# Second weight units of four streams, loaded and split into buffers of their own during the preceding stage

## The chip, the cores and the metric

One core of a Trainium2 chip runs the whole program in one launch. The metric is the device time in microseconds, the median of several runs. The engines named in the rows: PE is TensorE (matrix products), PEld its weight loads, DVE VectorE, ACT ScalarE, POOL GpSimd, SP SyncE (here it only issues DMAs).

## What is computed

Two blocks over 512 tokens of width 1024, in float32:

```python
h = x
for l in range(2):
    hn = rms_norm(h, norm_mix_pre[l])
    # l = 0: gated linear recurrence; l = 1: windowed attention with shared keys and values
    mixed = concat([y, memory_attention(mq, mk, mv)]) @ w_out[l]
    h = h + rms_norm(mixed, norm_mix_post[l])
    f = swiglu_ffn(rms_norm(h, norm_ffn_pre[l]), w_ffn_in[l], w_ffn_out[l])   # 1024 -> 2 x 2816 -> 1024
    h = h + rms_norm(f, norm_ffn_post[l])
    if l == 0:
        kv = rms_norm(h, norm_kv) @ w_kv_shared        # keys: first half, values: second half
# second block: modulation from silu(c) @ w_ada, then x_m, z, u = h @ w_in_2,
# an mLSTM and a Fourier mix, @ w_out_2, and a mixture of 16 experts
```

Every product is made of three passes in a rounded format: each operand is split into a high part (rounded) and a low part (the rest), and high x high, high x low and low x high are added.

## The kernel before

Weights stream through two slots. One half unit is 128 x 1024 numbers (512 KB). `load_half` (SyncE) brings it to `ring[s]`, `split_high` (ScalarE) rounds it to `weights_high`, `split_low` (VectorE) subtracts to get `weights_low`, and TensorE uses both in 24 matmuls of 512 columns. Slot s is 0 or 1; `landed[s]`, `high_done`, `split_done` and `used_done` are the semaphores, counted in one order over all halves: a slot is split again when the half before it in the same slot is used, and loaded again when that half is split. Each engine carries out its instructions in the order in which the Python code writes them.

`stream` runs a stage: units i with halves s = 0 and 1. For each half it writes load and split, then the evacuation of unit i - 1, then what is given as `beside(i, s)`, then TensorE's products, then, in the feed-forward stages, one or two sums of the modulation (`modulation_sum`, eight VectorE instructions on 128 x 128). `then` opens the next stage's first unit behind the last products.

The order of the stages: mixer 0 (its output rows by `mix_out`, 8 rows), feed-forward 0 (`ffn`: a stream of 22 units of w_ffn_in, then the stream of 22 rows of w_ffn_out in 11 units), the shared keys and values, queries of layer 1, attention, `mix_out` again, feed-forward 1, then z and u (4 units of w_in_2) and the rest of the second block. A stage of rows ends with `rows_root`: bank 0 is copied (`kept`), ScalarE squares the eight banks as `chunk_done` comes in, VectorE adds them, TensorE sums over features by one-column matmuls, and the root is spread. Then `Residual.chunks` adds the residual, and scales and splits X chunk by chunk, while TensorE makes the products of the next stage's first unit, both halves at once (the paired or fused first unit). `Residual.root` and `Residual.spread` make the next root; its copy `rstd` is what evacuations multiply by.

So the first unit of such a stage holds both slots until its end, and unit 1 can be split only then. In a feed-forward stage unit 1 is filled as a pair (`fused and i == 1`), the root is spread between its halves, and unit 0 is evacuated behind its second half (`evacuate(0, both)`: gate product on L1192, silu on L1196, product on L1203, high part on L1207, low part on L1210). Behind the keys the values use both slots in `token_products`, where tokens are the output rows, and then layer 1's first unit waits for them. For z and u, `both_columns` makes the first unit (L1651).

The modulation's weights go through `ring[2]` and `ring[3]` by GpSimd's queue (`modulation_load`), first at 175 us, and then each time one has been summed.

## Time and profile before

| what | value |
|---|---|
| median of 3 runs | 1953.93 us (1953.65 to 1957.99) |
| span of the profiled execution | 1947.3 us |
| TensorE busy | 1814.3 us (93%) |
| VectorE busy | 1216.2 us (62%) |
| ScalarE busy | 896.1 us (46%) |
| mean DMA rate | 149 GB/s |

The span runs from the first to the last instruction of one profiled execution; the device time of a run has some microseconds around it. Busy time of TensorE is not the same as work at its peak. The chain that ended last, followed back from the end, tells which engine's work the end hung on, and the timelines around a joint tell which wait ended last there. Matmuls are pipelined, so that their pitch is the distance of two starts and not the length of one.

### The profile page before, as it was taken

What the parts mean: (1) busy time and instruction counts of PE and PEld (TensorE: products, weight loads), DVE (VectorE), ACT (ScalarE), POOL (GpSimd) and SP (SyncE); (2) the same over time, 40 slices, a digit from 0 to 9 for tenths busy, and PEclk for the clock granted to TensorE, in tenths of its full rate; (3) what the DMA queues carried; (4) which work ended last, traced back from release to release, by engine and by line L of the source; (5) the groups of instructions that cost most, each with busy time, mean ns of one, the idle gap of its engine ahead of it and who ended that gap; (6) DMA issues with size and microseconds to landing.
All of it is one profiled execution on the core that took longest, in us unless ns stands there. A gap on an engine that the chain in (4) does not pass through costs nothing.

```text
span 1947.3 us, 25641 instructions
## 1 busy us (share of the span) xinstructions
PE 1814.3 (93%) x9201; PEld 1507.9 (77%) x9201; DVE 1216.2 (62%) x2170; ACT 896.1 (46%) x1452; POOL 125.7 (6%) x137
## 2 busy tenths in 40 slices
PE   7997999999999997899999999799987989999997
PEld 7875788888887865678888888678576878888885
DVE  3554668887323656456865532564575479889888
ACT  3446443222213445543223221342383368888885
POOL 1000000000000000000110000120000210110102
PEclk8898999999999998999999999799998879999999
DMA  4223225455333124024655423330011359999995
GB/s 150 87 76 115 87 64 142 134 145 147 107 96 96 44 65 184 23 65 137 182 159 149 119 93 97 112 89 22 21 67 66 108 222 377 395 385 370 386 372 187
DMA packets 203854, 289.32 MB, mean 149 GB/s; under 512 B 12332, under 2 KB 150548, under 8 KB 203636
## 3 DMA queue, kind: packets, MB, share of 16 engines
q1 hardware_dynamic: 188788, 239.56, 36.9%
q0 software_dynamic: 11920, 36.48, 6.1%
q10 hardware_dynamic: 3056, 12.06, 1.6%
q8 instruction: 59, 0.97, 0.2%
q14 instruction: 31, 0.25, 0.0%
HBM read 271.77 MB, written 21.53 MB: 151 GB/s over the span
## 4 chain that ended last, share of the span: by engine, by line
PE 85%; DVE 7%; ACT 6%; issue 1%; DMA 1%; POOL 0%; DVEq 0%; ACTq 0%; POOLq 0%
PE bank L200 23%; PE bank L202 23%; PE bank L201 23%; PE bank L69 11%; PE bank L654 2%; DVE weights_low L227 1%; PE bank L2195 1%; ACT weights_high L221 1%; DVE tmp L69 1%; DVE z_and_u L69 1%; DVE ring L69 1%; PE bank L1651 1%; ACT spare L69 1%; PE bank L2544 1%; PE bank L272 1%
## 5 line engine op out<-in xcount | busy, mean ns | idle before, releaser
L227 DVE TENSOR_TENSOR weights_low<-ring,weights_high 128x1024 fp32r<-128x1024 f32 x202 | 246.7, 1223 | 395.3 <-ACT weights_high L221 394.8
L200 PE MATMUL bank<-XH,weights_high 128*128 128x512 f32 x1056 | 423.2, 401 | 17.8 <-DVE weights_low L227 6.5
L202 PE MATMUL bank<-XH,weights_low 128*128 128x512 f32 x1056 | 415.6, 394 | 0.0
L201 PE MATMUL bank<-XL,weights_high 128*128 128x512 f32 x1056 | 415.2, 393 | 0.0
L221 ACT CAST weights_high<-ring 128x1024 fp32r<-128x1024 f32 x202 | 211.1, 1047 | 432.6 <-PE bank L202 422.8
L200 PEld LDWEIGHTS bank<-XH,weights_high 128*128 128x128 f32 x1056 | 200.8, 190 | 63.0 <-DVE weights_low L227 9.6
L202 PEld LDWEIGHTS bank<-XH,weights_low 128*128 128x128 f32 x1056 | 200.7, 190 | 43.4
L201 PEld LDWEIGHTS bank<-XL,weights_high 128*128 128x128 f32 x1056 | 201.1, 190 | 40.3 <-issue 0.5
L2235 DVE TENSOR_TENSOR XL<-ring,XH 128x1024 fp32r<-128x1024 f32 x144 | 169.8, 1219 | 11.7 <-ACT XH L2229 11.7
L2229 ACT CAST XH<-ring 128x1024 fp32r<-128x1024 f32 x144 | 145.2, 1048 | 0.6 <-PE bank L202 0.6
L69 DVE SCALAR_TENSOR_TENSOR squares<-ring,c_silu,squares 128x128 f32<-128x128 f32 x384 | 135.2, 352 | 13.6
L200 PE MATMUL bank<-hidden_high,weights_high 128*128 128x512 f32 x352 | 137.1, 390 | 0.0
L202 PE MATMUL bank<-hidden_high,weights_low 128*128 128x512 f32 x352 | 137.0, 389 | 0.0
L201 PE MATMUL bank<-hidden_low,weights_high 128*128 128x512 f32 x352 | 136.9, 389 | 0.0
L189 POOL DMA_DIRECT2D ring<-in_w_ada x48 | 42.5, 885 | 711.9 <-DVE squares L263 711.9
L2235 DVE TENSOR_TENSOR weights_low<-ring,weights_high 128x1024 fp32r<-128x1024 f32 x72 | 86.0, 1216 | 0.0
L1196 ACT ACTIVATE tmp<-tmp 128x512 f32<-128x512 f32 x44 | 27.8, 632 | 109.2 <-DVE tmp L1192 109.1
L202 PEld LDWEIGHTS bank<-hidden_high,weights_low 128*128 128x128 f32 x352 | 66.1, 188 | 13.8
L201 PEld LDWEIGHTS bank<-hidden_low,weights_high 128*128 128x128 f32 x352 | 66.1, 188 | 13.8
L200 PEld LDWEIGHTS bank<-hidden_high,weights_high 128*128 128x128 f32 x352 | 66.1, 188 | 13.4
L200 PE MATMUL bank<-weights_high,gathered_high 128*128 128x256 f32 (+1 forms) x216 | 70.8, 328 | 3.6 <-DVE weights_low L2235 1.8
L2229 ACT CAST weights_high<-ring 128x1024 fp32r<-128x1024 f32 x72 | 74.1, 1053 | 0.0
(506 smaller groups left out, 3263.2 us busy)
## 6 DMA issues: line engine op xcount, KB each, us to landing
ring<-in_w_ffn_in SPq DMA_DIRECT2D x88, 512.0 KB, 4.7
ring<-in_w_gate SPq DMA_DIRECT2D x72, 512.0 KB, 5.4
ring<-in_w_up SPq DMA_DIRECT2D x72, 512.0 KB, 7.3
ring<-in_w_down SPq DMA_DIRECT2D x72, 512.0 KB, 5.9
ring<-in_w_ada POOLq DMA_DIRECT2D x48, 512.0 KB, 4.7
ring<-in_w_ffn_out SPq DMA_DIRECT2D x44, 512.0 KB, 3.6
ring<-in_w_out SPq DMA_DIRECT2D x24, 512.0 KB, 3.6
slot_output<-expert_out SPq DMA_DIRECT2D x18, 512.0 KB, 6.7
```

The source lines that it names most:

```text
L69: op(*args, **kw).then_inc(self.line.sem, 1)
L189: queue.eng.dma_start(dst, src).then_inc(ln.sem, 16)
L200: PE.matmul(out_ap, w_h, x_h, start=first, stop=False, skip_group_check=True)
L201: PE.matmul(out_ap, w_h, x_l, start=False, stop=False, skip_group_check=True)
L202: return PE.matmul(out_ap, w_l, x_h, start=False, stop=last, skip_group_check=True)
L221: S.copy(wh[:, s, :], ring[s][:, :]).then_inc(high_done.sem, 1)
L227: V.tensor_tensor(wl[:, s, :], ring[s][:, :], wh[:, s, :].bitcast(F32), ALU.subtract).then_inc(split_done.sem, 1)
L272: t = PE.matmul(bank[7][:, 2 * n + j:2 * n + j + 1], ada_acc(n, j), ones[:, 0:1], start=True, stop=True, skip_group_check=True)
L654: return PE.matmul(bank[s][:, cols], w[:, s, k * P:(k + 1) * P], x[:, k, cols], start=start, stop=stop, skip_group_check=True)
L1196: S.activation(sg, sg, ACT.Silu).then_inc(silu_done.sem, 1)
L2229: S.copy(high[s], raw[q]).then_inc(l_high.sem, 1)
L2235: V.tensor_tensor(low[s], raw[q], high[s].bitcast(F32), ALU.subtract).then_inc(l_split.sem, 1)
```

## The change

A class `Early` holds a pair of buffers (high and low, at a fixed address) for unit 1 of a stream, or, for the values, for their only unit. Its `load` puts the two halves into `ring[2]` and `ring[3]` on SyncE, and its `split` rounds and subtracts one half behind the waits given. `stream` takes `early`: unit 1 is then not filled, its products read these buffers, and unit 2 is opened in the slots at once (in the feed-forward stages ahead of the two evacuations of unit 0). The waits on slots count per slot (`slot_used`, `slot_split`), since uses no longer alternate. Where and behind what it is done:

- feed-forward 0: loaded ahead of mixer 0's output rows, split at (3, 0) and (3, 1), the last two of its eight rows. The first two modulation loads move behind these splits.
- values: loaded at (8, 0) of feed-forward 0's rows, split at (10, 0) and (10, 1), the last two of 22. Modulation loads 20 and 21 move to the next item.
- feed-forward 1: loaded ahead of mixer 1's output rows, split at (2, 0) and (2, 1).
- z and u: loaded at (8, 0) of feed-forward 1's rows behind `used_done.now()`, split at (9, 1) and (10, 0); the additions of the position stay in their place (given as `beside` now and no longer as an evacuation).

In `rows_root`, `split_low(0)` moves ahead of the additions of the squares.

```diff
-            g = high_done.n
             S.wait_ge(landed[s].sem, landed[s].n)
-            if g >= 2:
-                S.wait_ge(used_done.sem, g - 1)
+            if slot_used[s]:
+                S.wait_ge(used_done.sem, slot_used[s])
...
+            slot_split[s] = split_done.n
+
+        def slots_used(*each):
+
+            for s in each:
+                used_done.n += 1
+                slot_used[s] = used_done.n
+
+        def wait_slots(*each):
+
+            PE.wait_ge(split_done.sem, max(slot_split[s] for s in each))
+
+        class Early:
+
+
+            def __init__(self, name, src, unit, at):
+                self.src, self.unit = src, unit
+                self.high, self.low = (nc.alloc_sbuf_tensor_at(f"{name}_unit_{x}", [P, 2, HALF], F32R, offset=at + 2 * HALF * 4 * n)
+                                       for n, x in enumerate(("high", "low")))
+                self.high_line, self.split_line = line(f"{name}_high_done"), line(f"{name}_split_done")
+
+            def load(self, *after):
+                sp.need(*after)
+                for s in range(2):
+                    ap, view = self.src(self.unit, s)
+                    load(sp, landed[2 + s], view(ring[2 + s][:, :]), ap)
+
+            def split(self, s, *after):
+                act.need(*after)
+                S.wait_ge(landed[2 + s].sem, landed[2 + s].n)
+                S.copy(self.high[:, s, :], ring[2 + s][:, :]).then_inc(self.high_line.sem, 1)
+                self.high_line.n += 1
+                V.wait_ge(self.high_line.sem, self.high_line.n)
+                V.tensor_tensor(self.low[:, s, :], ring[2 + s][:, :], self.high[:, s, :].bitcast(F32),
+                                ALU.subtract).then_inc(self.split_line.sem, 1)
+                self.split_line.n += 1
...
-                    if i == 0 and s in opened:
+                    if s in opened:
                         opened.remove(s)
                     elif fused and i == 1:
                         if s == 0:
-                            fill_half(src, i, 0)
-                            fill_half(src, i, 1)
+                            if not early:
+                                fill_half(src, i, 0)
+                                fill_half(src, i, 1)
                             fused.root()
-                    else:
+                    elif not (early and i == 1):
...
+                            wait_slots(0, 1)
                             paired()
-                            used_done.n += 2
+                            slots_used(0, 1)
+                    elif early and i == 1:
+                        PE.wait_ge(early.split_line.sem, s + 1)
+                        products(i, s, False, early).then_inc(used_done.sem, 1)
+                        used_done.n += 1
+                        if not fused:
+                            open_half(src, s, 2)
                     else:
-                        PE.wait_ge(split_done.sem, used_done.n + 1)
+                        wait_slots(s)
                         products(i, s, i == 0).then_inc(used_done.sem, 1)
-                        used_done.n += 1
+                        slots_used(s)
                     if fused and i == 1:
                         if s == 0:
                             fused.spread()
                         else:
                             for both in range(2):
+                                if early:
+                                    open_half(src, both, 2)
                                 evacuate(0, both, used_done.n - 2)
...
-                            if n + 2 < 48:
+                            if n + 2 < 48 and n + 2 not in (20, 21):
...
+                PE.wait_ge(early.split_line.sem, 2)
+            else:
+                wait_slots(0, 1)
+            w_h, w_l = (early.high, early.low) if early else (wh, wl)
...
+                split_low(0)
             added, squared = {}, {}
             for c in range(KC):
                 if c == 0:
@@ -564,7 +617,6 @@
                     added[c] = vec.do(V.tensor_tensor, total, total, squares[c % 4], ALU.add,
                                       after=[squared[c], added[c - 1]])
             if next_src:
-                split_low(0)
...
+            if i == 3:
+                early.split(s, used_done.now(), vec.line.now())
         load(pool, tables_landed, con[:, P:], I["constants"][:, P:], after=[used_done.now()])
         pool.need(used_done.now())
+        unit_at = 191616
+        early = Early("first_ffn", ffn_src(0), 1, unit_at)
+        early.load(used_done.now())
+        spread = mix_out(I["w_out"][0], ffn_src(0), row_order, row_ready, row_part)
+        G.wait_ge(early.split_line.sem, 2)
         modulation_load(0)
         modulation_load(1)
-        spread = mix_out(I["w_out"][0], ffn_src(0), row_order, row_ready, row_part)
         a_ctx.close()
-        spread = ffn(0, Residual(column["mix_post0"], spread, column["ffn_pre0"], True), columns_src(I["w_kv_shared"]))
+        value_src = columns_src(I["w_kv_shared"], base=KV_HEADS * DH)
+        values_early = Early("values", value_src, 0, 204416)
+
+        def split_values(i, s):
+            if (i, s) == (8, 0):
+                values_early.load((ada_summed, ada_sums[19]))
+            if i == 10:
+                values_early.split(s, used_done.now())
+        spread = ffn(0, Residual(column["mix_post0"], spread, column["ffn_pre0"], True), early, columns_src(I["w_kv_shared"]),
+                     split_values)
...
-        fill_half(value_src, 0, 0)
-        fill_half(value_src, 0, 1)
...
-        spread = mix_out(I["w_out"][1], ffn_src(1), row_order, row_ready)
+        early = Early("second_ffn", ffn_src(1), 1, unit_at)
+        early.load(used_done.now(), values_early.split_line.now())
+
+        def split_early(i, s):
+            if i == 2:
+                early.split(s, used_done.now())
+        root_table()
+        spread = mix_out(I["w_out"][1], ffn_src(1), row_order, row_ready, split_early)
+        G.wait_ge(early.split_line.sem, 2)
+        modulation_load(20)
+        modulation_load(21)
...
+        zu_early = Early("z_and_u", zu_src, 1, 149632)
+
+        def positions_and_early(i, s):
+            if i:
+                add_position(i - 1, s, None)
+            if (i, s) == (8, 0):
+                zu_early.load(used_done.now(), (ada_summed, ada_summed.n))
+            if i in (9, 10):
+                if (i, s) in ((9, 1), (10, 0)):
+                    zu_early.split(2 * i + s - 19, used_done.now())
+        spread = ffn(1, Residual(column["mix_post1"], spread, column["ffn_pre1"], True), early, zu_src, positions_and_early)
...
-            stream(4, zu_src, columns_products(T, XH, XL), zu_and_context, then=opener(in2_src), paired=both_columns)
+            stream(4, zu_src, columns_products(T, XH, XL), zu_and_context, then=opener(in2_src), paired=both_columns, early=zu_early)
```

## Rows read from the trace of the kernel before

**Rows 1.** The page's chain that ended last: shares of the span by engine.

```profile
PE 85%; DVE 7%; ACT 6%; issue 1%; DMA 1%; POOL 0%; DVEq 0%; ACTq 0%; POOLq 0%
```

**Rows 2.** The chain in order of time, first feed-forward: start us, us, what.

```profile
256.16 0.79 PE bank L69 x8
```

**Rows 3.** Timeline of PE, first feed-forward: start, us, instruction, [idle before <-releaser].

```profile
261.45 0.95 PE L69 MATMUL bank<-ones,squares 128*128 128x1 f32 x8
262.71 0.50 PE L200 MATMUL bank<-XH,weights_high 128*128 128x512 f32 x1 [0.31 <-DVE weights_low L227]
...
276.03 0.39 PE L202 MATMUL bank<-XH,weights_low 128*128 128x512 f32 x1
277.23 0.50 PE L200 MATMUL bank<-XH,weights_high 128*128 128x512 f32 x1 [0.81 <-DVE weights_low L227]
...
288.05 0.39 PE L202 MATMUL bank<-XH,weights_low 128*128 128x512 f32 x1
```

**Rows 4.** VectorE's timeline and its waits (in total, times, longest), 271.5 to 287.9.

```profile
271.60 0.69 DVE L1192 TENSOR_TENSOR tmp<-bank,rstd 128x512 f32<-128x512 f32 x1 [7.31 <-ACT rstd L69]
...
286.62 1.22 DVE L227 TENSOR_TENSOR weights_low<-ring,weights_high 128x1024 fp32r<-128x1024 f32 x1
...
DVE hidden_low L1210 <- ACT hidden_high L1207: 1.4, 2, 0.7
DVE tmp L1203 <- ACT tmp L1196: 1.3, 1, 1.3
DVE weights_low L227 <- ACT weights_high L221: 0.3, 1, 0.3
```

**Rows 5.** Timeline of ScalarE, VectorE and PE around the first mixer's root.

```profile
228.39 1.05 ACT L221 CAST weights_high<-ring 128x1024 fp32r<-128x1024 f32 x1 [4.39 <-PE bank L202]
229.01 0.69 DVE L69 COPY spare<-bank 128x512 f32<-128x512 f32 x1 [3.76 <-PE bank L202]
...
233.70 1.49 DVE L69 TENSOR_TENSOR tmp<-tmp,squares 128x512 f32<-128x512 f32 x2
...
235.62 1.31 PE L69 MATMUL bank<-ones,tmp 128*128 128x1 f32 x8
```

**Rows 6.** Around the values: timeline (long rows) and chain (short rows).

```profile
650.56 0.95 PE L69 MATMUL bank<-ones,squares 128*128 128x1 f32 x8
653.26 0.55 PE L200 MATMUL bank<-weights_high,XH 128*128 128x256 f32 x1 [1.76 <-DVE weights_low L227]
...
660.69 1.29 DVE L69 TENSOR_TENSOR rotated<-bank,const_tables 128x512 f32<-128x512 f32 x2
...
667.00 0.13 PE bank L202
...
669.57 0.50 PE bank L200
```

**Rows 7.** The chain around z and u.

```profile
1275.95 2.73 PE bank L1651 x12
...
1281.13 0.50 PE bank L200
```

**Rows 8.** Second feed-forward's last rows: ScalarE's timeline, one load's landing, and a stretch.

```profile
1207.31 1.05 ACT L221 CAST weights_high<-ring 128x1024 fp32r<-128x1024 f32 x1 [4.39 <-PE bank L202]
...
DMA to landing us min/median/max: 3.8/3.8/3.8
...
1228.00:1228.50 0.50, 0.50 (x4) 0.42 (x3) 0.00 (x0) 0.00 (x0) 0.00 (x0) 1.00 1.01 307
```

**Rows 9.** Stretches: us, busy (x) of PE, PEld, DVE, ACT, POOL, granted clock, DMA share, GB/s.

```profile
263.70:267.10 3.40, 3.40 (x9) 2.62 (x9) 0.56 (x3) 0.00 (x0) 0.00 (x0) 0.52 0.85 235
653.00:656.20 3.20, 2.94 (x14) 2.97 (x15) 3.20 (x7) 3.20 (x6) 0.00 (x0) 0.52 0.89 264
881.50:884.70 3.20, 3.20 (x9) 2.49 (x8) 0.69 (x3) 0.00 (x0) 0.00 (x0) 0.50 0.81 228
667.20:669.50 2.30, 0.78 (x2) 0.00 (x0) 1.22 (x2) 2.29 (x4) 0.00 (x0) 1.00 0.00 0
1278.70:1281.10 2.40, 1.33 (x6) 0.76 (x5) 1.23 (x1) 2.33 (x3) 0.00 (x0) 1.00 0.00 0
```

More of the change, by code:

```diff
@@ L288, in opener, with stream @@
             return lambda s: open_half(src, s)
-        def stream(units, src, products, evacuate=None, side=None, then=None, fused=None, beside=None, paired=None):
+        def stream(units, src, products, evacuate=None, side=None, then=None, fused=None, beside=None, paired=None, early=None):
             pending = []
@@ L379, in columns_products, with products @@
         def columns_products(n, xh, xl, to=0, ready=None):
-            def products(i, s, first):
-                w_h = wh[:, s, :].rearrange("p (k n) -> p k n", k=KC)
-                w_l = wl[:, s, :].rearrange("p (k n) -> p k n", k=KC)
+            def products(i, s, first, halves=None):
+                high, low = (halves.high, halves.low) if halves else (wh, wl)
+                w_h = high[:, s, :].rearrange("p (k n) -> p k n", k=KC)
+                w_l = low[:, s, :].rearrange("p (k n) -> p k n", k=KC)
                 b = to + 4 * (i % 2) + s
@@ L393, in columns_products, with token_products @@
             return products
-        def token_products(tiles, xh, xl, to=0, between=None):
+        def token_products(tiles, xh, xl, to=0, between=None, early=None):
             for a in range((tiles + 1) // 2):
                 pe.need(*bank_free[to + a])
-            PE.wait_ge(split_done.sem, used_done.n + 2)
+            if early:
+                PE.wait_ge(early.split_line.sem, 2)
+            else:
+                wait_slots(0, 1)
+            w_h, w_l = (early.high, early.low) if early else (wh, wl)
             for m in range(tiles):
@@ L404, in token_products @@
                     x_h, x_l = xh[:, k, m * P:(m + 1) * P], xl[:, k, m * P:(m + 1) * P]
-                    last = three_pass(dst, x_h, x_l, wh[:, :, k * P:(k + 1) * P], wl[:, :, k * P:(k + 1) * P],
+                    last = three_pass(dst, x_h, x_l, w_h[:, :, k * P:(k + 1) * P], w_l[:, :, k * P:(k + 1) * P],
                                       k == 0, k == KC - 1)
@@ L409, in token_products @@
             last.then_inc(used_done.sem, 2)
-            used_done.n += 2
+            if early:
+                used_done.n += 2
+            else:
+                slots_used(0, 1)
         def rows_products(units, xh, xl, ready=None, order=None, tokens=None, between=None):
@@ L693, in chunks @@
                             pe.need(*bank_free[0], *bank_free[1])
-                            PE.wait_ge(split_done.sem, used_done.n + 2)
+                            wait_slots(0, 1)
                         if j == 0:
@@ L717, in chunks @@
                             one_pass(1, wh, XL, k, stop=True).then_inc(used_done.sem, 1)
-                            used_done.n += 2
+                            slots_used(0, 1)
                     if j and (self.next_gain is None or j < KC - 1):
@@ L788, in products @@
                         pe.need(*bank_free[0], *bank_free[1])
-                        PE.wait_ge(split_done.sem, used_done.n + 2)
+                        wait_slots(0, 1)
                     pe.need(low[k])
@@ L795, in products @@
                         last.then_inc(used_done.sem, 2)
-                        used_done.n += 2
+                        slots_used(0, 1)
                 for k in range(KC):
@@ L1174, in program, with ffn @@
                      [[], []] + [[n, n + 1] for n in range(20, 36, 2)] + [[n] for n in range(36, 48)])
-        def ffn(l, residual, next_src, beside=None):
+        def ffn(l, residual, early, next_src, beside=None):
             ctx = ExitStack()
@@ L1213, in ffn @@
             rows = rows_src(I["w_ffn_out"][l])
-            stream(FC, ffn_src(l), columns_products(T, XH, XL), evacuate, side=ada_steps[l], then=opener(rows), fused=residual)
+            stream(FC, ffn_src(l), columns_products(T, XH, XL), evacuate, side=ada_steps[l], then=opener(rows), fused=residual, early=early)
             root_table()
-            stream(FC // 2, rows, rows_products(FC // 2, HH, HL, low_part), beside)
+            stream(FC // 2, rows, rows_products(FC // 2, HH, HL, low_part), None, beside=beside)
             spread = rows_root(root_floor[:, :], next_src)
@@ L1474, in add_position @@
             x_ready[k] = [vec.do(V.tensor_tensor, x, x, e, ALU.add, after=x_ready[k])]
-        spread = ffn(1, Residual(column["mix_post1"], spread, column["ffn_pre1"], True), zu_src, add_position)
+        zu_early = Early("z_and_u", zu_src, 1, 149632)
[8 more added lines that the diff above has]
+        spread = ffn(1, Residual(column["mix_post1"], spread, column["ffn_pre1"], True), early, zu_src, positions_and_early)
         mem_ctx.close()
```

10 lines of the change are left out of this document (4 added, 6 removed).

## Prediction

> **What bounds the kernel now.** I read the page's chain first. TensorE carries 85% of it [rows 1], so a change pays only where it shortens a wait of TensorE, and costs wherever it makes one. Then I read the four joints that the change touches, in order of time, each in the chain and in the timelines of TensorE, VectorE and ScalarE.
>
> First feed-forward stage. The paired first unit ends with eight one-column matmuls at 261.45, which take 0.79 us in the chain [rows 2, 3]. The second unit could start at 262.24; it starts at 262.71, released by VectorE's low part of its weights [rows 3]. Wait: 0.47 us. A second one follows before unit 2: the last matmul starts at 276.03 and the next at 277.23 against a normal pitch of 0.23, so 0.97 us [rows 3]. The second feed-forward stage, 617.9 us later, has the same two.
>
> Values. Eight one-column matmuls start at 650.56 and take 0.79; the values begin at 653.26: 1.91 us. They end at 667.13, and the queries of layer 1 begin at 669.57, because their weights share the two slots: 2.44 us [rows 6].
>
> z and u. The paired unit ends at 1278.68 and the next starts at 1281.13: 2.45 us [rows 7].
>
> Together these are 0.47 + 0.97, twice, 1.91 + 2.44 and 2.45, or 9.7 us. That is the ceiling of the plain story, before the clock.
>
> **What becomes of each wait.** The first unit of a wait goes entirely: its weights were split rows earlier, when VectorE and ScalarE were mostly idle. Values: -1.91. z and u: -2.45, and 0.1 for a pipeline start (the first matmul after a wait takes 0.34 to the next start instead of 0.23). For the queries, VectorE's last rotation ends at 660.69 + 1.29 = 661.98 [rows 6] and comes earlier by about 1.5, as two splits and the wait are gone in front of it. Two splits of 1.2 each put the weights at 662.9. TensorE ends the values at about 667.13 - 1.91 - 1.5 of clock (below) = 663.7 at the earliest. So the work is hidden, barely, and -2.44 - 0.1 holds.
>
> The 0.97 before unit 2 does not go. **VectorE is next.** In units 2 to 17 each unit has two splits, three passes of the gate and sixteen sums for the modulation. From the end of the root's copy at 271.57, VectorE runs to the end of the low part of unit 3, 286.62 + 1.22 = 287.84, so 16.27 us, and waits only 1.3 + 1.4 + 0.3 = 3.0 of them [rows 4]. TensorE starts unit 3 at 288.05 + 0.23 = 288.28 [rows 3]: 0.4 behind VectorE. The change leaves this list of work whole and only puts the two splits of unit 2 ahead of the gate and of the product of unit 0. Replayed from the copy's end with the same durations: ScalarE's split ends at 1.1 (VectorE waits 1.1), low part to 2.3, gate to 2.9, then silu to 3.6 and ScalarE's second split to 4.5, which VectorE must have (1.6 more), and twice 0.7 for the hidden halves. That is 4.1 of waiting and 13.3 of work: 17.35. TensorE, free of its own wait, asks for unit 3 at 15.7 and gets it at 17.35; before it had it at 288.28 - 271.57 = 16.71. So the second wait moves to unit 3 and grows: +0.64 in place of -0.97, in both stages. After that VectorE gains 0.2 a unit, and nothing repeats. Bounds: -1.1 (all hidden) and +1.6. I take +0.64, as it is a replay of the rows.
>
> **The last row before a root.** In the first mixer's output rows and in the first feed-forward's rows, the second half is split during the last row; its wait (`used_done.now()`) ends when the row before is done. That is 228.39 in the mixer, exactly when ScalarE now splits for the next stage and just before VectorE copies bank 0 at 229.01 [rows 5]. The early low part is ahead of this copy on VectorE: 228.39 + 1.05 + 1.23 = 230.67 with handovers, so the copy comes 1.6 late. The squares wait for it, and the five sums for the squares; the moved `split_low(0)` stands between (1.2, until now in idle time). ScalarE, once released, squares at 0.5 a piece instead of at TensorE's pace of 0.68, and the last sum ends near 236.4 instead of 233.70 + 1.49 = 235.19. The last eight one-column matmuls start at 235.62 now [rows 5] and at about 236.8 then: **+1.2**, and the root's path is bare from there. Bounds 0 and 1.6. This is paid in the first mixer and before the values. In the second mixer (`i == 2`) and for z and u the splits lie rows earlier: nothing, and the moved `split_low(0)` fits in VectorE's wait of about 1.2 behind the copy.
>
> **The queue that is blocked.** For z and u the two loads are issued at the half (8, 0) of 11 x 2, behind `used_done.now()`: SyncE stands until row 15 of 22 is done, 1207.31 by ScalarE's split that waits for the same event [rows 8]. Row 17's load, so far issued some 8 us earlier, stands behind them. TensorE has 5.44 us of row 16 left, then needs row 17. A lone load of this kind lands in 3.8 us, and its bytes run at 307 GB/s, 1.7 us for 0.5 MB [rows 8]. Three in a row: 3.8 + 1.7 + 1.4 = 6.9 at most, 6.5 if starts overlap. Landed at 1214.0, ScalarE's and VectorE's splits add 2.35, row 17 is ready at 1216.4 and was due at 1212.7: **+3.7 us**, a wait that takes the place of the one removed. Bounds: 1.4 (a lone load's time, the others free) and 3.9. The values' loads at their (8, 0) wait only for sums long done, and the two mixers' loads wait for products that are done too: no cost. On GpSimd the first modulation loads go from 175 to about 231 and are first read at 277: hidden.
>
> By the Trainium skill (DMA: Bandwidth & Descriptors, "Queues, rings and completion order"), descriptors of one queue on one DMA engine are consumed in ring order, which speaks against this edit: row 17's bytes can't overtake. No row of before shows three loads queued on SyncE, so it is open until the run.
>
> **The clock.** After the waits the granted clock was 0.52 for 3.4 us in the first feed-forward stage, 0.52 for 3.2 at the values, and 0.50 for 3.2 in the second feed-forward stage; in the waits at 667 and 1278 it stayed 1.00 [rows 9]. A fall costs 3.4 x 0.48 = 1.6, 1.5 and 1.6. With less idle time ahead it may not fall, but the one-column matmuls stay, and in the feed-forward stages only 0.47 us of idle goes. I count half: -2.35. The new stall of 3.7 may make it fall: half of 1.6, +0.8. Together -1.55, bounds -4.7 and +1.6.
>
> The Trainium skill (TensorE: Matmul & The Clock Gate, Part 1) says that the lower level is the default, idle time leads to it and sustained activity lifts it. By that rule alone the three falls would all be gone (the clock term -4.7); the rows agree at the three falls and not at 667 and 1278.
>
> **The sum.** First mixer and feed-forward: +1.2 - 0.47 + 0.64 = +1.4. Values: +1.2 - 1.91 - 2.54 = -3.25. Second feed-forward: -0.47 + 0.64 = +0.2. z and u: -2.55 + 3.7 = +1.15. Sum -0.5; with the clock -2.1. Against the profiled span of 1947.3: 1945.2. Outside the span lie 6.6 us to the median of 1953.93, which the change leaves alone: **1951.8 us**.
>
> **The rivals.**
> 1. VectorE is not next: both second waits go as drawn (-1.1 each, not +0.64). -3.5, so 1948.3. For it: VectorE's replay has 1.6 us of margin to be wrong in. Against: 3.0 us idle of 16.3 in the rows. Chance 0.12.
> 2. The row stall is small or absent, since the loads overlap: up to -3.7, 1948.1. For it: the range of a load's landing. Against: even a lone load gives 1.4. Chance 0.13.
> 3. The clock doesn't fall at all: -3.15, 1948.7. By the skill's rule above this is what happens. With rival 1 or 2 it reaches 1945. Chance 0.12.
> 4. On the other side: the blocked queue decides. The stall at row 17 takes the clock down with it, the three falls stay: -0.5 + 1.6 = +1.1, 1955.0; it ends slower once stall and fall cost more than 4.2 us together at unchanged clock elsewhere. Nothing in before is as long as this stall except the wait at 184, which was at 0.50 already. Chance 0.15.
> 5. It does nothing, each wait being replaced at once by another (1954): 0.05.
>
> The forecast itself has 0.43, with its own range 1949.5 to 1954. The range over the cases is 1944.5 to 1957: below, two of rivals 1 to 3 together; above, rival 4 with the root's delay at its bound. About 0.3% (5.9 us) is what a measurement can tell from none. Faster by more (under 1948.1) takes rivals 1 to 3 about to the half and mostly in pairs: 0.25. Slower by more: 0.08. Within: 0.67.
>
> **What would show it.** Values and z and u: no wait ahead of the early unit, queries' first matmul right behind the values. Feed-forward stages: the wait at unit 2 gone and one at unit 3, released by VectorE's low part. Root: VectorE's copy of bank 0 about 1.6 later than the last row's start allows. Second feed-forward's rows: TensorE idle ahead of row 17 for 3 to 4 us, released by the low part, itself by ScalarE behind a landing. If row 17 shows no wait, the DMA step is wrong; if unit 3 shows none, the replay is; if the stretches after the removed waits are still at 0.5, the clock term is.

## The result, and the profile after

| | before | after |
|---|---|---|
| median | 1952.56 us (1947.48 to 1957.99, 20 runs) | 1959.41 us (1952.03 to 1965.84, 20 runs) |
| profiled span | 1947.3 us | 1960.4 us |
| end of the opening stage in the profile (GpSimd issues the load of the tables) | 175.3 us | 181.6 us |
| from there to the end | 1772.0 us | 1778.8 us |

The ratio is 1.0031 (95%: 1.0020 to 1.0042): slower, by 6.1 us of 1952.56, where 1951.8 and a fall of 2.1 were forecast. A second comparison of the same two kernels gave 1.0063 (1.0044 to 1.0082), so the size of the loss is less certain than its sign.

Half of the 13.1 us between the spans is not the change's. The opening stage, which it doesn't touch, took 6.3 us longer in this execution, at the half clock for longer. That is why the stages below are measured from its end.

The page of after, as in the table ahead of the prediction:

```profile
span 1960.4 us, 25644 instructions
PE 1825.1 (93%) x9201; PEld 1516.0 (77%) x9201; DVE 1215.4 (62%) x2170; ACT 894.7 (46%) x1452; POOL 125.4 (6%) x137
```

**The two feed-forward stages.** After, first feed-forward: timeline of PE (start, us, instruction, [idle before <-releaser]), its waits (total, times, longest), and VectorE's timeline ahead of unit 3.

```profile
270.47 0.95 PE L69 MATMUL bank<-ones,squares 128*128 128x1 f32 x8
271.28 0.47 PE L200 MATMUL bank<-XH,first_ffn_unit_high 128*128 128x512 f32 x1
...
295.82 0.50 PE L200 MATMUL bank<-XH,weights_high 128*128 128x512 f32 x1 [1.57 <-DVE weights_low L226]
...
PE bank L200 <- DVE weights_low L226: 1.6, 1, 1.6
...
294.55 1.22 DVE L226 TENSOR_TENSOR weights_low<-ring,weights_high 128x1024 fp32r<-128x1024 f32 x1
```

The early unit starts without a wait, where [rows 3] had 0.31 of idle. The wait ahead of unit 2 (277.23 there) is gone, and one of 1.57 us has come ahead of unit 3. Both stages show the same.

**The first mixer's root.** After: ScalarE, VectorE and PE.

```profile
234.57 1.05 ACT L259 CAST first_ffn_unit_high<-ring 128x1024 fp32r<-128x1024 f32 x1 [3.44 <-PE bank L202]
...
235.66 1.23 DVE L262 TENSOR_TENSOR first_ffn_unit_low<-ring,first_ffn_unit_high 128x1024 fp32r<-128x1024 f32 x1 [3.08 <-ACT first_ffn_unit_high L259]
236.80 0.69 DVE L69 COPY spare<-bank 128x512 f32<-128x512 f32 x1
...
241.13 1.49 DVE L69 TENSOR_TENSOR tmp<-tmp,squares 128x512 f32<-128x512 f32 x2
...
241.25 1.02 PE L69 MATMUL bank<-ones,tmp 128*128 128x1 f32 x8 [1.28 <-ACT tmp L69]
242.13 1.64 PE L69 MATMUL bank<-ones,spare 128*128 128x1 f32 x8
243.64 1.85 PE L69 MATMUL bank<-ones,tmp 128*128 128x1 f32 x8
```

Against [rows 5], counted from ScalarE's split (228.39 there, 234.57 here), the copy of bank 0 comes 1.61 later and VectorE's last sum 1.25 later. TensorE's last eight one-column matmuls come 1.84 later and take 1.85 in place of 1.31. The half clock begins at the same place in both kernels, 7.8 us behind ScalarE's split (236.2 there, 242.4 here). In before it came within the third group of eight, now it comes within the second. The second group of before:

```profile
234.72 1.03 PE L69 MATMUL bank<-ones,spare 128*128 128x1 f32 x8
```

**Values.** After, PE: the last squares of the keys' stage, the first product of the values, and the first of layer 1.

```profile
660.53 0.95 PE L69 MATMUL bank<-ones,squares 128*128 128x1 f32 x8
661.34 0.36 PE L200 MATMUL bank<-values_unit_high,XH 128*128 128x256 f32 x1
...
673.82 1.02 PE L69 MATMUL bank<-proj_b,const_tables 128*128 128x512 f32 x2
674.28 0.80 PE L200 MATMUL bank<-x_high_b,weights_high 128*128 128x512 f32 x1
```

Both gaps of [rows 6], ahead of 653.26 and ahead of 669.57, are gone: 12.94 us from the values' first product to layer 1's, in place of 16.31. The second gap had not begun at 667.13, as the chain has it: PE's timeline of before shows two more matmuls, of the keys' rotation, and then 1.59 us of idle time.

```profile
666.95 1.02 PE L69 MATMUL bank<-proj_b,const_tables 128*128 128x512 f32 x2
669.57 0.50 PE L200 MATMUL bank<-x_high_b,weights_high 128*128 128x512 f32 x1 [1.59 <-DVE weights_low L227]
```

**Row 17 of the second feed-forward stage.** After: SyncE's timeline, the chain that ended last (start, us, what), and PE's timeline.

```profile
1211.41 1.00 SPq L189 DMA_DIRECT2D ring<-in_w_in  x2
...
1212.46 5.99 DMA ring<-in_w_ffn_out
1218.48 1.05 ACT weights_high L220
1219.55 1.24 DVE weights_low L226
...
1220.83 0.50 PE L200 MATMUL bank<-hidden_high,weights_high 128*128 128x512 f32 x1 [4.01 <-DVE weights_low L226]
```

TensorE stood for 4.01 us. Row 17's load, issued behind z and u's two, landed after 5.99 us, at 1218.45, where a lone one took 3.8 [rows 8]; the two ahead of it had landed at 1215.41 and 1217.19.

**z and u.** The PE timeline of after around the joint; then that of before, which [rows 7] had shown only as a chain.

```profile
1291.16 0.39 PE L1735 MATMUL bank<-XL,weights_high 128*128 128x512 f32 x1
1291.38 0.39 PE L200 MATMUL bank<-XH,z_and_u_unit_high 128*128 128x512 f32 x1
```

```profile
1278.51 0.39 PE L1651 MATMUL bank<-XH,weights_high 128*128 128x512 f32 x1
...
1279.65 0.39 PE L1651 MATMUL bank<-XL,weights_high 128*128 128x512 f32 x1
1281.13 0.50 PE L200 MATMUL bank<-XH,weights_high 128*128 128x512 f32 x1 [1.09 <-DVE weights_low L227]
```

The gap is closed, but it had been 1.25 us (1281.13 - 1279.65 - 0.23) and not 2.45.

**The clock.** After: stretches behind the three joints that had been at half clock [rows 9], and behind the stall of row 17 (us, busy (x) of PE, PEld, DVE, ACT, POOL, granted clock, DMA share, GB/s).

```profile
272.00:275.50 3.50, 3.50 (x17) 2.84 (x17) 0.12 (x1) 0.00 (x0) 0.00 (x0) 1.00 0.00 0
...
658.00:661.00 3.00, 3.00 (x22) 2.75 (x23) 0.00 (x0) 0.00 (x0) 0.00 (x0) 1.00 0.00 0
885.00:889.00 4.00, 4.00 (x22) 3.41 (x23) 0.34 (x2) 0.26 (x1) 0.00 (x0) 1.00 0.00 0
...
1222.50:1225.90 3.40, 3.40 (x10) 2.64 (x10) 0.00 (x0) 0.00 (x0) 0.00 (x0) 0.57 0.76 266
```

All three falls are gone, and a new one stands behind row 17. (The second line lies ahead of the values' first product at 661.34; no half clock is granted from 645.1 to 747.5.) But the stretch at half clock that begins in each root is longer: 13.7 us in place of 10.2 in the first mixer, 10.2 in place of 6.8 before the values, 10.2 in place of 6.8 in the second mixer. Over all stages behind the opening, the stretches at half clock add up to 171.6 us in before and to 178.6 in after (181.4 in its second profile).

**Stage by stage.** Joints are the first product of a paired unit, and layer 1's first product; "again" is the profile of the second comparison, "forecast" the prediction's sum laid on the same joints. Differences are taken before rounding.

| from ... to | before | after | again | difference | forecast |
|---|---|---|---|---|---|
| opening's end to the first feed-forward's unit 0 | 66.7 | 68.9 | 68.9 | +2.2 | +1.2 |
| to the keys' unit 0 | 389.1 | 390.9 | 390.8 | +1.8 | +0.6 |
| to layer 1 (values) | 38.5 | 32.9 | 32.8 | -5.6 | -5.2 |
| to the second feed-forward's unit 0 | 190.5 | 190.5 | 190.6 | +0.1 | 0 |
| to the end of its rows | 379.2 | 384.6 | 384.5 | +5.3 | +3.9 |
| root, to z and u | 28.3 | 28.3 | 28.4 | 0 | 0 |
| to the end | 679.7 | 682.8 | 681.8 | +3.0 | -2.55 |
| sum | 1772.0 | 1778.8 | 1777.8 | +6.8 | -2.1 |

Half of the last stage's 3.0 us can be placed. The last root, ahead of the router, has no early split near it, and its rows are as before up to the clock; from the last matmul of its rows to the router's first it takes 9.59 us in place of 8.08. PE's last group in it, after and then before:

```profile
1549.42 1.63 PE L69 MATMUL bank<-ones,tmp 128*128 128x1 f32 x8
```

```profile
1537.13 1.03 PE L69 MATMUL bank<-ones,tmp 128*128 128x1 f32 x8
```

Two executions of one kernel (after and its second profile, e4_all_three and e11_all_again below) agree within 1 us a stage behind the opening, and within 1.0 in the sum. The opening itself (174.6 to 182.0 over all profiles) is most of what single spans differ by.

### The profile page after: what moved, and what is told of

Read it like the earlier page. It is cut to its first block, busy times and chain, and to the rows that moved or that the text cites. A ratio compares the mean times of both kernels' runs of the same rounds, so it can differ in the third digit from the quotient of the medians.

```text
span 1960.4 us, 25644 instructions
## 1 busy us (share of the span) xinstructions
PE 1825.1 (93%) x9201; PEld 1516.0 (77%) x9201; DVE 1215.4 (62%) x2170; ACT 894.7 (46%) x1452; POOL 125.4 (6%) x137
## 4 chain that ended last, share of the span: by engine, by line
PE 83%; DVE 8%; ACT 6%; issue 1%; DMA 1%; POOL 0%; SPq 0%; DVEq 0%; ACTq 0%; POOLq 0%
PE bank L200 23%; PE bank L202 22%; PE bank L201 22%; PE bank L69 12%; PE bank L706 2%; DVE weights_low L226 1%; PE bank L2279 1%; DVE squares L69 1%; DVE tmp L69 1%; ACT squares L69 1%; ACT weights_high L220 1%; PE bank L1735 1%; DVE z_and_u L69 1%; DVE ring L69 1%; ACT tmp L69 1%
## 5 line engine op out<-in xcount | busy, mean ns | idle before, releaser
L226 DVE TENSOR_TENSOR weights_low<-ring,weights_high 128x1024 fp32r<-128x1024 f32 x194 | 236.8, 1223 | 378.2 <-ACT weights_high L220 378.1
L200 PE MATMUL bank<-XH,weights_high 128*128 128x512 f32 x1008 | 404.4, 401 | 17.0 <-DVE weights_low L226 6.3
L202 PE MATMUL bank<-XH,weights_low 128*128 128x512 f32 x1008 | 397.2, 394 | 0.0
L201 PE MATMUL bank<-XL,weights_high 128*128 128x512 f32 x1008 | 396.7, 394 | 0.0
L220 ACT CAST weights_high<-ring 128x1024 fp32r<-128x1024 f32 x194 | 202.7, 1048 | 389.1 <-PE bank L202 375.6
L200 PEld LDWEIGHTS bank<-XH,weights_high 128*128 128x128 f32 x1008 | 192.0, 190 | 59.8 <-DVE weights_low L226 8.8
L202 PEld LDWEIGHTS bank<-XH,weights_low 128*128 128x128 f32 x1008 | 191.9, 190 | 41.6
L201 PEld LDWEIGHTS bank<-XL,weights_high 128*128 128x128 f32 x1008 | 192.2, 191 | 38.4 <-issue 0.5
L2319 DVE TENSOR_TENSOR weights_low<-ring,weights_high 128x1024 fp32r<-128x1024 f32 x72 | 86.0, 1217 | 0.0
L2313 ACT CAST weights_high<-ring 128x1024 fp32r<-128x1024 f32 x72 | 74.0, 1053 | 0.0
```

Of the source, the lines that this page charges most:

```text
L200: PE.matmul(out_ap, w_h, x_h, start=first, stop=False, skip_group_check=True)
L201: PE.matmul(out_ap, w_h, x_l, start=False, stop=False, skip_group_check=True)
L202: return PE.matmul(out_ap, w_l, x_h, start=False, stop=last, skip_group_check=True)
L220: S.copy(wh[:, s, :], ring[s][:, :]).then_inc(high_done.sem, 1)
L226: V.tensor_tensor(wl[:, s, :], ring[s][:, :], wh[:, s, :].bitcast(F32), ALU.subtract).then_inc(split_done.sem, 1)
L2313: S.copy(high[s], raw[q]).then_inc(l_high.sem, 1)
```

## The experiments

The first four ran in one comparison (33 runs of before, median 1950.65), the next four in another (24 runs, 1952.32), the three behind them in a third (15 runs, 1948.82), the last in a fourth (16 runs, 1951.09). The first two comparisons ran on one chip, the third and the fourth on one other each. All numbers of stages are from the kernel's own profile. One profile's sum behind the opening and the median time can part by several microseconds, as in e1_free_sync, e3_vector_order and e8_low_back.

**e1_free_sync: row 17 without the queue's wait.**

```diff
-                zu_early.load(used_done.now(), (ada_summed, ada_summed.n))
+                zu_early.load((ada_summed, ada_summed.n))
```

> One edit to the changed kernel: the two loads for z and u no longer wait for used_done.now(), only for the last modulation sum, so that SyncE goes on at once to row 17's load. Theory 1 (the delays placed by the change are its loss): the 4.0 us wait at row 17 and the 3.4 us at the half clock behind it (1.6 us) go, so the time is 4.0 to 5.6 us below the changed kernel's, that is 0.0 to 0.1% above before instead of 0.31%. Theory 2 (the length of the low-clock stretches around the roots and the opening decides, and the wait at row 17 is only a part of what moves them): less than 2 us come back.

Measured: 1951.89 us (12 runs), ratio 1.0002 (0.9987 to 1.0018). No wait of TensorE is left in the rows, and the stretch that held the fall has the full clock:

```profile
1221.80:1225.40 3.60, 3.60 (x18) 2.98 (x17) 0.00 (x0) 0.58 (x1) 0.00 (x0) 1.00 0.49 146
```

The stage takes 378.0 us in place of 384.6. One wait on SyncE's queue, of a load that nobody needed for 80 us, cost stall and fall together, 5.6 us by the rows (4.01 and 1.6), and the ratio is 0.29 points better than the changed kernel's first one. The profile behind the opening is 1767.9 us long, 10.9 less than after and 4.1 less than before, since the layer 1 stage (188.5), z and u's root (27.5) and the last stage (681.3) are shorter than in after too; the times don't show that part.

**e2_clear_roots: the last row before a root free of early splits.**

```diff
-            if i == 3:
-                early.split(s, used_done.now(), vec.line.now())
+            if (i, s) in ((2, 1), (3, 0)):
+                early.split(1 - s, used_done.now(), vec.line.now())
...
-            if i == 10:
-                values_early.split(s, used_done.now())
+            if (i, s) in ((9, 1), (10, 0)):
+                values_early.split(1 - s, used_done.now())
```

> One edit to the changed kernel: the second half of the first feed-forward's and of the values' early unit is split one row earlier, at (2, 1), (3, 0) and at (9, 1), (10, 0), so that nothing stands on VectorE ahead of the copy of bank 0. Theory 1: both roots come 1.2 us earlier, and the first low-clock stretch behind them is not lengthened: 2.4 to 5 us below the changed kernel. Theory 2: the roots come earlier in the trace, but the low stretches last to their next step anyway, so under 2 us in the time. In either case row 17's wait of 4 us stays.

Measured: 1952.11 us (12 runs), ratio 1.0001 (0.9987 to 1.0015). From the last row's last matmul to the next stage's first product the first mixer takes 8.87 us (before 8.63, after 10.95), the values' root 8.75 (7.57, 10.22). VectorE's copy is back in place, 0.63 behind ScalarE's split as in [rows 5]:

```profile
228.05 0.69 DVE L69 COPY spare<-bank 128x512 f32<-128x512 f32 x1 [1.61 <-PE bank L202]
...
234.65 1.56 PE L69 MATMUL bank<-ones,tmp 128*128 128x1 f32 x8
```

Behind the opening the profile takes 1773.4 us in place of 1778.8. So the root's delay is the early split in the last row, and it costs more than the 1.2 of the prediction. Before the values 1.2 us more than in before stay, for which no cause is shown.

**e3_vector_order: the gate of unit 0 ahead of the second split.**

```diff
-                            for both in range(2):
-                                if early:
-                                    open_half(src, both, 2)
-                                evacuate(0, both, used_done.n - 2)
+                            if early:
+                                load_half(src, 2, 0)
+                                load_half(src, 2, 1)
+                                split_high(0)
+                                evacuate(0, 0, used_done.n - 2)
+                                split_low(0)
+                                split_high(1)
+                                evacuate(0, 1, used_done.n - 2)
+                                split_low(1)
+                                opened.update((0, 1))
```

> One edit to the changed kernel: in the fused unit 1 the gate of unit 0 goes ahead of unit 2's first low part on VectorE, and its product and hidden halves ahead of the second low part. Replayed from the rows, VectorE waits 2.8 us of its list and not 4.1, so that unit 3 starts 16.0 us behind the root's copy and not 17.3: the 1.6 us wait of TensorE at unit 3 falls to about 0.3 in both feed-forward stages, 2.6 us in all. Theory 1 expects these 2.6 us in the time. If VectorE is not what unit 3 waits for, the wait stays at 1.6.

Measured: 1956.14 us (12 runs), ratio 1.0016 (1.0004 to 1.0029). Unit 3 follows without a wait, and from unit 1 to unit 3 it takes 23.05 us, where after has 24.54 and before 25.57:

```profile
291.52 0.39 PE L202 MATMUL bank<-XH,weights_low 128*128 128x512 f32 x1
291.98 0.50 PE L200 MATMUL bank<-XH,weights_high 128*128 128x512 f32 x1
```

Twice 1.5 us, and the ratio is 0.15 points better, though the intervals overlap. The wait at unit 3 came from VectorE's order and not from the amount of its work. (The edit also issues both loads of unit 2 first; VectorE's waits in this stretch are for ScalarE alone.) Behind the opening, however, this profile is 1778.9 us long, as after (1778.8): the layer 1 stage takes 192.9 in place of 190.5, and the values' 34.0 in place of 32.9.

**e4_all_three: the three edits together.**

> The three edits of the other kernels of this call together. Theory 1: the sum, 9 to 13 us below the changed kernel, so 3 to 7 us (0.15 to 0.35%) below before. Theory 2: at or above before.

Measured: 1941.73 us (10 runs), ratio 0.9949 (0.9932 to 0.9967); opening's end to the end 1763.3 us. The three alone had gained 0.29, 0.30 and 0.15 points against the changed kernel's first ratio, 0.74 in all; together they gain 0.82. The agreement is looser than it looks, as the changed kernel's own ratio moved by 0.32 points between comparisons. This version beats both kernels.

**e5_no_zu and e6_no_ffn: what the early units are worth in it.** The first leaves z and u's early unit out of e4_all_three, the second those of the two feed-forward stages.

> The kernel with all three edits, without the early unit for z and u (its load, its split and its buffers gone; unit 1 of this stream is filled in the slots again). It measures that part alone. By TensorE's own timeline the wait before z and u's second unit is 1.25 us and not the 2.45 of the prediction, so theory 1 says 1.4 us slower than with it, under what these rounds can tell; the prediction's term says 2.55 slower. Theory 2 (clock phases decide) gives no bound.

> The kernel with all three edits, without the early units of both feed-forward stages; those for the values and for z and u stay. The feed-forward stages then go as before the change: their second unit starts 0.47 us later, 3.4 us at the half clock come back in it (1.6 us), TensorE waits 0.97 ahead of unit 2. Theory 1: 2.5 us more for each stage, 5 us in all (0.26%) slower than with all three edits. If the fall of the clock would be gone without them too: under 3 us.

Measured: 1944.13 us (12 runs), ratio 0.9959 (0.9945 to 0.9973), and 1945.54 us (7 runs), 0.9961 (0.9945 to 0.9976). Neither differs from e4_all_three beyond the intervals. The traces do tell. Without z and u's unit the wait is back, and the stretch from z and u to the end takes 679.7 in place of 678.3, as expected:

```profile
1280.46 0.50 PE L200 MATMUL bank<-XH,weights_high 128*128 128x512 f32 x1 [1.10 <-DVE weights_low L226]
```

Without the feed-forward units the stretch from unit 1 to unit 3 takes 25.6 us again in the first stage (23.0 with them), and the falls of the clock are back in both stages; behind the opening the profile takes 1769.3 us, 5.9 more, where 5 were expected:

```profile
266.00:269.40 3.40, 3.40 (x10) 2.67 (x11) 1.38 (x3) 0.04 (x1) 0.00 (x0) 0.62 0.61 180
881.00:884.40 3.40, 3.40 (x10) 2.70 (x9) 0.92 (x3) 0.00 (x0) 0.00 (x0) 0.53 0.74 210
```

**e7_extra_vector: a root made late by itself.** Before, with one VectorE instruction ahead of each root's copy of bank 0; its result is not used.

```diff
+            V.tensor_tensor(sq[:, :, :], X[:, 0:2, :], X[:, 0:2, :], ALU.mult)
             m0 = vec.do(V.tensor_copy, kept, bank[0][:, :])
```

> The kernel before with one more VectorE instruction of 128 x 1024 (1.2 us, its result is not used) ahead of each copy of bank 0 in rows_root, which runs five times. It measures the disputed cost by itself. Linear theory (the prediction's): each root comes 0.5 to 1.2 us later, 2.5 to 6 us in all. Clock theory: the idle time of TensorE grows past the point where its clock falls earlier, so that the one-column matmuls behind it run at the half clock too, and the cost per root is about 2 us: 8 to 11 us in all. Hidden: under 1.5.

Measured: 1951.94 us (12 runs), ratio 1.0000 (0.9987 to 1.0013). Of the three sizes the smallest came, but the delay was not hidden. PE at the first root, and the stretch of the first feed-forward that had the fall:

```profile
239.96 1.02 PE L69 MATMUL bank<-ones,tmp 128*128 128x1 f32 x8 [0.87 <-ACT tmp L69]
240.85 1.36 PE L69 MATMUL bank<-ones,spare 128*128 128x1 f32 x8
242.07 1.84 PE L69 MATMUL bank<-ones,tmp 128*128 128x1 f32 x8
...
264.00:267.40 3.40, 3.40 (x24) 3.06 (x24) 1.58 (x3) 1.25 (x2) 0.00 (x0) 1.00 0.00 0
```

The copy is 1.15 us late and the root takes 10.26 us in place of 8.63, the next three 1.5 to 1.9 us more too, the last 1.1: 7.8 in all. But from unit 1 to unit 3 both feed-forward stages take 24.0 in place of 25.57: their fall is gone, though TensorE waits ahead of units 1 and 2 as before (0.32 and 0.80 us idle). There the root's own stretch at half clock is the longer one, 13.7 us in place of 10.2, as in after. Behind the opening the profile is only 3.4 us longer, with 165.1 us at half clock in place of 171.6; the time allows 2.5. Why the clock gave this back is open.

**e8_low_back: e4_all_three with `split_low(0)` back behind the additions of the squares.**

> The kernel with all three edits, with split_low(0) moved back behind the additions of the squares, as before the change. Theory 1: the instruction fits in VectorE's wait of 1.2 us behind the copy of bank 0, so both places cost the same: within 0.15% of the kernel with all three edits, and the additions start 1.95 us behind the copy in both.

Measured: 1944.38 us (6 runs), ratio 0.9953 (0.9937 to 0.9969), the same as e4_all_three within the intervals. The times show no worth of that move, either way. Its profile is 5.3 us longer behind the opening, 4.7 of them from z and u to the end (682.95 in place of 678.3), where again the last root runs at half clock (9.62 us).

**e10_double_vector: the same delay twice as long.**

```diff
+            x0 = vec.do(V.tensor_tensor, sq[:, :, :], X[:, 0:2, :], X[:, 0:2, :], ALU.mult)
+            vec.do(V.tensor_tensor, sq[:, :, :], X[:, 0:2, :], X[:, 0:2, :], ALU.mult, after=[x0])
             m0 = vec.do(V.tensor_copy, kept, bank[0][:, :])
```

> The kernel before with two VectorE instructions of 128 x 1024 ahead of the copy of bank 0 at each root, 2.46 us each time, where the run with one had 1.23 and showed no loss in the time. Theory (a late root costs what it is late, less a fall of the clock that it saves): root segments of 11 to 12 us in place of 8.6 and 7.5, some 2.5 to 3.5 us more at each of five, less 1.6 us at each of two falls behind that stay away: the time 8 to 14 us (0.4 to 0.7%) above the kernel before. Rival (a late root is returned whole by the clock): within 2.5 us of the kernel before.

Measured: 1968.85 us (6 runs), ratio 1.0096 (1.0072 to 1.0119), or +18.7 us, above the 14 expected. PE at the first root, and a stretch of the first feed-forward:

```profile
241.18 1.84 PE L69 MATMUL bank<-ones,tmp 128*128 128x1 f32 x8 [2.47 <-ACT tmp L69]
242.88 1.85 PE L69 MATMUL bank<-ones,spare 128*128 128x1 f32 x8
244.58 1.84 PE L69 MATMUL bank<-ones,tmp 128*128 128x1 f32 x8
...
272.20:275.60 3.40, 3.40 (x10) 2.67 (x9) 0.96 (x3) 0.00 (x0) 0.00 (x0) 0.57 0.74 202
```

With 2.4 us of delay TensorE idles 2.47 us ahead of the sums, so that all three groups run at half clock (5.5 us in place of 3.4). The first root takes 13.15 us, 4.5 more, and the fall in the feed-forward stays. The next three take 3.5 to 5.0 us more. A late root is no linear cost. In the first mixer and its feed-forward, 1.15 us of delay costs 1.6 in the root and 0.8 in the products up to unit 1, more of which run at half clock, and a fall that stays away returns 1.6: 0.8 is left at unit 3. 2.4 us of delay costs 4.5 in the root, and 3.9 is left.

**e9_first_root: only the first mixer's root cleared in the changed kernel.** The first hunk of e2_clear_roots alone.

> The changed kernel with only the first mixer's early split moved away from the last row: first half at (3, 0) and second at (2, 1) in the order of the clear-roots run; the values' split stays in the last row. Theory (the late root costs about 2.2 us in the first mixer): the first root segment falls from 10.9 to about 8.9 us, the values' stays at 10.2, and the time falls by 2 us (0.1%) against the changed kernel beside it. Rival (the root's lateness is given back later by the clock, as the run with the extra VectorE instruction suggests): the root segment shortens and the time stays within 0.5 us.

**a0_after_again: the changed kernel beside it.**

> The changed kernel, unaltered, on the same chip and beside the same runs of the kernel before as the two above. If the loss of 0.31% belongs to the kernel, the ratio lies between 1.002 and 1.005. If it belonged to the chip or the hour of the first comparison, it lies within 1.000 to 1.0015.

Measured: 1955.86 us (10 runs), ratio 1.0036 (1.0023 to 1.0048), and 1961.29 us (6 runs), 1.0063 (1.0044 to 1.0082). The first root takes 9.06 us in place of 10.99, as expected, but the values' takes 11.18 in place of 10.26, which was not: nothing there is different but when it comes. Behind the opening the profile is 0.6 us shorter (1777.2 and 1777.8), near the rival's forecast; the medians differ by 5.4, but the intervals overlap, so the run settles no size for the first root. That the changed kernel is slower holds in both comparisons; its 0.63% lies above the expected 0.5% and is not explained.

**e11_all_again: e4_all_three in another comparison.**

> The kernel with all three repairs (no wait on products for z and u's loads, root rows free of early splits, gate ahead of the second split in the feed-forward stages), unaltered, in another comparison, since the changed kernel itself gave 1.0031 in one and 1.0063 in another. If its gain of 0.5% belongs to the kernel: a ratio of 0.992 to 0.998. If it belonged to the comparison: 0.9985 or above.

Measured: 1944.08 us (11 runs), ratio 0.9960 (0.9945 to 0.9974). The gain is the kernel's: 0.4 to 0.5%. Its profile is 1763.4 us long behind the opening, 1763.3 in e4_all_three, while the spans are 1938.0 and 1945.3.

## Why the prediction was wrong

Point by point, in its own steps:

- **What becomes of each wait: right in kind, two sizes misread.** The waits ahead of the early units and the one behind the values went. For z and u the gap was read in the chain [rows 7], whose 1278.68 is where the chain leaves slot 0's last product; TensorE went on with slot 1's to 1279.65. The gap in PE's timeline, 1.25 with 1.09 of idle time, was the number to take. With the 0.1 for the start the term is -1.4 in place of -2.55, and e5_no_zu against e4_all_three shows 1.4. The gap behind the values was read in the chain too: two matmuls of 1.02 us stood in it. From them to layer 1's first product before has 2.62 us and after 0.46, so that term is -2.2 in place of -2.54; the products of the values ran 1.2 us faster without their fall, which hides it in the stage's sum.
- **VectorE is next: right.** From the root's copy to unit 3's low part the replay gave 17.35; the row gives 294.55 + 1.22 - 278.52 = 17.25. The wait at unit 3 is 1.57 us, and e3_vector_order removes it by the order alone. The 0.47 us ahead of unit 1 went too, but the chunks before it took as much longer (20.75 to unit 1, 20.73 before), as more of them ran at half clock.
- **The last row before a root: mechanism right, size wrong.** VectorE was late by 1.25, as forecast (1.2). The term took the one-column matmuls at their durations of [rows 5]. They took 1.64 and 1.85 in place of 1.03 and 1.31, since the clock fell in the second group and no longer in the third: +2.3 in the first mixer and +2.65 before the values, in place of twice +1.2. e10_double_vector shows the same at a larger size.
- **The queue that is blocked: right, just above its upper bound.** 4.01 against 3.7, bounds 1.4 and 3.9. (The lower bound doesn't follow from its own terms: 1207.31 + 3.8 + 2.35 - 1212.7 = 0.8.) By the Trainium skill (DMA: Bandwidth & Descriptors, "Queues, rings and completion order") the descriptors of a ring are consumed in order on each DMA engine; the trace agrees with it, as row 17's load landed last of the three, after 5.99 us. Three loads that only shared the bandwidth could have given the same time. The fall behind the stall came in both profiles of the changed kernel, where the prediction had counted half of it: +1.6.
- **The clock: the three falls went, and the term still failed. This and z and u's gap are the steps that made the forecast wrong.** The term stood at -1.55. It counted half of 4.7 back. All of it came back at the joints, but the roots took longer stretches at half clock, about as much in all (3.5 + 3.4 + 3.4 = 10.3 us longer, against 3.4 + 3.2 + 3.2 = 9.8 us of falls in [rows 9]). And behind z and u, where the change does nothing but close the gap, after needs 682.8 and 681.8 us in place of 679.7, with 6.4 us more at half clock (8.9 in the second profile); e4_all_three, with the same code there, needs 678.3 and 678.5. Which earlier shift decides that isn't shown. Behind the opening as a whole, half clock grew by 7.0 us and by 9.8 in the second profile; at the prediction's price of 1.6 us for 3.4 that is, as an estimate, +3.3 to +4.6 where the term had -1.55. The prediction had no term for the roots' stretches nor for the stages behind: the last stage with its mis-read gap is 5.5 of the 8.9 us between forecast and result, by the table. The other parts are +1.0 and +1.2 in the two stages with the early splits in the last row, +1.4 at row 17's stage, and -0.3 elsewhere.
- **The rivals.** Number 4 (stall and fall of the blocked queue decide) named the right side and the right mechanism, with 1955.0 for its price; it lacked the roots. Alone it would have been no loss: e2_clear_roots has stall and fall and is level with before. It also had the three falls stay, and they went. Of number 3 the three falls at the joints did not happen, but the one behind row 17 did, and there was no gain. 0.08 for slower by over 0.3% was too little, since the roots were priced at rows with the full clock and the fall behind the stall at half.

The rule of the Trainium skill (TensorE: Matmul & The Clock Gate, Part 1) that idle time leads to the lower level, by which closing the gaps ends the falls, agrees with after and with e6_no_ffn. It doesn't suffice: in e7_extra_vector the same fall went while the idle time ahead of it stayed. Nor is a longer stretch in the root what removes the fall in after: e4_all_three has 10.2 us in the first mixer's, as in before, and no fall.

## What to carry to other kernels

Work that is taken off one joint must not land in the row ahead of another: keep the last row ahead of a root free of it, order it behind nothing that the queue's next load doesn't need, and write the engine's list so that what feeds TensorE's critical input comes ahead of what is only opened early. Here that turned +0.3% into -0.4 to -0.5% with the same early units. Size a gap in the bounding engine's own timeline and not in the chain. Where only short matmuls follow a new wait, cost them at the half clock and not at the rows' durations.

## What the runs showed of the hardware that was not expected

- The cost of a delay ahead of a root depends on the granted clock behind it: 1.15 us late gave no measurable loss over five roots (ratio 1.0000, though the five roots were 7.8 us longer), 2.4 us late gave 18.7 us, as groups of eight one-column matmuls took 1.84 us in place of 1.02.
- The clock's falls move as a pattern. The layer 1 stage, whose work is the same, took 190.5 us in after and 193.9 in e4_all_three; between 740 and 806 us the half clock lasts 20.5 us in the one and 27.3 in the other. These two kernels repeated their own figures within 1 us a stage in a second profile.
- The opening stage's time at half clock changes between executions of one kernel: e4_all_three and e11_all_again differ by 7.3 us at its end and by 0.1 us behind it. A span alone compares two kernels no better than that.
